# Squared tiles summed on VectorE, the first stage's products in column tiles, an earlier q copy, and head roots spread from rows

## The chip, the cores and the metric

The kernel runs on one core of one Trainium2 chip. The metric is the device time in microseconds (us) of one execution. Five engines have instruction streams of their own: PE (TensorE, matrix products), ACT (ScalarE), DVE (VectorE), POOL (GpSimd) and SP (SyncE, which here only issues transfers). They meet through semaphores: `then_inc` counts one up when an instruction is done, `wait_ge` holds an engine's stream until the count is reached.

## The reference

A sequence of 512 tokens of width 1024 goes through one large block and two smaller layers, all in float32:

```python
# block 1
mx = split(silu(c) @ w_ada + b_ada, 6); mc = the same of c_ctx
hx = modulate(rms_norm(x, g_pre_mix), mx[0], mx[1]);  hc = the same of ctx (256 tokens)
yx = concat(mlstm heads, silu(layer_norm(conv(ga * sigmoid(gb))))) @ w_out + b_out
x  = x + mx[2] * rms_norm(yx);  x = x + mx[5] * rms_norm(moe(modulate(rms_norm(x), mx[3], mx[4])))
# block 2, layers 0 (even) and 1 (odd)
for layer in range(2):
    x = x + mixer(rms_norm(x))            # rope attention, 8 pairs of heads; the odd one takes
                                          # rms_norm of each pair's output over 128 channels
    x = x + conv_ffn(rms_norm(x))         # (silu(gate) * val) @ w_down
return rms_norm(x, final_norm)
```

An `rms_norm` over the width needs, for each token, the sum of 1024 squares; the layer norm of the convolution needs a mean and a variance over 512 channels.

## The kernel before, in words

The program is a chain of stages with a barrier between them, and nothing of a stage's compute starts before the barrier; weights that `m.early` fetched are the exception. Activations lie turned: `m.x` is 8 tiles of 128 channels by 512 tokens, so a sum over channels is a matrix product with a constant matrix (`inv_d`, `inv_c`) that also spreads the result over all partitions. An ordinary weight product splits both sides in a high and a low part (`w_high`, `w_low`, `h_high`, `h_low`) and runs three passes of a faster format (`passes`); the sums of squares are plain float32 products, which the trace records as two matmuls each.

Five places matter here.

- `prologue` (lines 291 to 390). ACT squares the eight tiles of `x` and `ctx`; PE sums each pair as it comes (line 327). Then `product(n)`, four times, multiplies `silu_c` (two columns, for `c` and `c_ctx`) with a 2 MB quarter of `w_ada` that SP fetches (line 316), ACT copies the two rows out (line 363), `turn(n)` turns them into columns (line 340), and DVE adds the bias (line 381). Meanwhile DVE takes the reciprocal and scales `x` to `unit` tiles (line 376).
- `project_in` (lines 418 to 713). The last block of weight products is `rows("o")` in four chunks; after chunk 1 PE runs `mean` (line 518) and after chunk 2 `variance` (line 524), four float32 products each over the convolution's tiles `acc` and their centred squares `gb`.
- `Tail` (lines 2043 to 2083). Both `mix_out` (the output projection of an attention layer, eight columns `j` of 24 matmuls) and the second part of `conv_ffn` (eight columns of 30 matmuls) add their product to `m.x[:, j]` on DVE. `on_scalar` squares that tile, `on_tensor` adds the square into bank 6 or 7 two columns later, and `root` takes the square root at the stage's end. `split` says that the stage also prepares `hs.high` and `hs.low` for the next one.
- `mix_out` with `heads` (the odd layer). PE spreads the reciprocal roots `head_rstd` over the partitions (line 2186), DVE multiplies (`norm`, line 2152), ACT and DVE split, and only after all eight spreads does PE start the weight products (line 2198).
- `attention` (lines 2231 to 2605). Before the loop over eight pairs of heads the stage makes q, k and v of pair 0. All three projections write the same bank `BP`, so the projection of k waits until ACT has copied q out (`take(0, 0)`, line 2451, which signals `raw_done`). ACT has first to pass `act.wait_ge(w_in[1], 16)`, the arrival of the weights of the next pair, 1.5 MB that SP issues behind the 1 MB `amask`.

## Time and profile before

| | |
|---|---|
| median of 3 runs | 2568.27 us (2567.26 to 2576.4) |
| the profiled execution | 2567.37 us, of which the span from first to last instruction is 2565.6 us |
| busy in the span | PE 2357.6 us (92%), PE weight loads 1759.0 (69%), DVE 1535.2 (60%), ACT 1173.2 (46%), POOL 300.2 (12%) |
| mean granted TensorE clock | 0.955 of full speed (2.4 GHz; the lower level is 1.2 GHz) |

In the table of stretches each row gives the length, the busy time of each engine with its count of instructions, the granted clock, the busy share of the DMA engines and GB/s. A timeline row gives start, duration, engine, line, operation, output<-inputs, shapes and count; what stands in brackets is how long the engine had been idle before and who released it.

### The profile page before, as it was taken

How to read it: one execution, taken by the hardware profiler on the slowest of the kernel's cores; microseconds unless marked ns; L12 is line 12 of the kernel's file. 1: busy time of each engine (PE TensorE's matmuls, PEld its weight loads, DVE VectorE, ACT ScalarE, POOL GpSimd, SP SyncE). 2: the span in 40 equal slices, each digit the busy share in tenths (PEclk: the TensorE clock that was granted, in tenths of full speed). 3: DMA queues.
4: the chain of work that ended last, by engine and by line, in shares of the span. 5: the costliest groups of instructions: out<-in, count | busy, mean ns of one | idle time of the engine just before them, and what ended most of it. 6: DMA issues, size and time to landing. Idle time of an engine off the chain costs nothing. (4 is left out here: it accounts for less than half of the span.)

```text
span 2565.6 us, 30607 instructions
## 1 busy us (share of the span) xinstructions
PE 2357.6 (92%) x10686; PEld 1759.0 (69%) x10686; DVE 1535.2 (60%) x2414; ACT 1173.2 (46%) x1853; POOL 300.2 (12%) x223
## 2 busy tenths in 40 slices
PE   7998888899999999973899899999989979999997
PEld 2875664677677767752666578888767757888885
DVE  4974544777777777748455457637536544773663
ACT  4314442566666666644354434324334433442341
POOL 0000000121122112210343000000013410000000
PEclk9997899899999999996999899999999989999999
DMA  6203504799999999956421222222232101323221
GB/s 250 99 25 136 198 13 170 281 364 360 346 359 361 353 352 357 376 213 242 156 74 41 66 91 96 88 95 98 82 132 73 66 20 63 123 90 107 98 79 69
DMA packets 86753, 427.39 MB, mean 167 GB/s; under 512 B 19728, under 2 KB 19856, under 8 KB 51056
## 3 DMA queue, kind: packets, MB, share of 16 engines
q1 hardware_dynamic: 67344, 392.32, 41.9%
q0 software_dynamic: 19296, 33.60, 3.6%
q8 instruction: 66, 1.08, 0.2%
q14 instruction: 47, 0.39, 0.0%
HBM read 415.36 MB, written 38.80 MB: 177 GB/s over the span
## 5 line engine op out<-in xcount | busy, mean ns | idle before, releaser
L1796 DVE TENSOR_TENSOR w_gu_low<-raw,w_gu_high 128x1024 fp32r<-128x1024 f32 x264 | 322.6, 1223 | 121.9 <-ACT w_gu_high L1745 110.0
L1745 ACT ACTIVATE w_gu_high<-raw 128x1024 fp32r<-128x1024 f32 x264 | 279.8, 1060 | 108.7 <-PE banks L1701 107.8
L2718 PE MATMUL banks<-h_high,w_high 128*128 128x512 f32 x704 | 275.8, 392 | 6.8 <-DVE w_low L2818 6.8
L2718 PE MATMUL banks<-h_high,w_low 128*128 128x512 f32 x704 | 275.5, 391 | 0.0
L2718 PE MATMUL banks<-h_low,w_high 128*128 128x512 f32 x704 | 275.3, 391 | 0.0
L1713 PE MATMUL banks<-raw,act_t 128*128 128x512 f32 x528 | 237.6, 593 | 0.9 <-ACT act_t L1768 0.9
L1701 PE MATMUL banks<-w_gu_high,x_t_high 128*128 128x512 f32 x528 | 214.1, 406 | 2.0 <-DVE x_t_low L1803 2.0
L1701 PE MATMUL banks<-w_gu_high,x_t_low 128*128 128x512 f32 x528 | 208.0, 394 | 0.0
L1701 PE MATMUL banks<-w_gu_low,x_t_high 128*128 128x512 f32 x528 | 207.6, 393 | 0.0
L2745 ACT ACTIVATE w_high<-raw 128x2048 fp32r<-128x2048 f32 (+2 forms) x74 | 124.1, 1677 | 157.4 <-PE banks L2728 152.7
L2782 DVE TENSOR_TENSOR w_low<-raw,w_high 128x2048 fp32r<-128x2048 f32 (+2 forms) x74 | 148.3, 2004 | 59.6 <-ACT w_high L2745 59.5
L1713 PEld LDWEIGHTS banks<-raw,act_t 128*128 128x128 f32 x528 | 95.2, 190 | 95.8 <-issue 94.7
L2718 PEld LDWEIGHTS banks<-h_high,w_high 128*128 128x128 f32 x704 | 133.2, 189 | 36.1 <-issue 8.4
L2757 ACT ACTIVATE conv<-mix,vec 128x512 f32<-128x512 f32 x88 | 71.9, 817 | 183.2 <-DVE mix L2797 183.2
L2718 PEld LDWEIGHTS banks<-h_low,w_high 128*128 128x128 f32 x704 | 133.2, 189 | 27.7
L2718 PEld LDWEIGHTS banks<-h_high,w_low 128*128 128x128 f32 x704 | 133.0, 189 | 27.9
L1874 POOL DMA_INDIRECT x_rows<-h_rows,token_i x68 | 70.4, 1036 | 679.1 <-DVE token_i L1824 678.7
L2728 PE MATMUL banks<-hidden_high,w_high 128*128 128x512 f32 x352 | 141.7, 402 | 2.5 <-DVE w_low L2782 2.5
L2728 PE MATMUL banks<-hidden_high,w_low 128*128 128x512 f32 x352 | 137.2, 390 | 0.0
L2728 PE MATMUL banks<-hidden_low,w_high 128*128 128x512 f32 x352 | 137.0, 389 | 0.0
L1763 ACT ACTIVATE y_block<-banks 128x512 f32<-128x512 f32 x132 | 78.8, 597 | 86.4 <-PE banks L1713 85.7
L1701 PEld LDWEIGHTS banks<-w_gu_high,x_t_low 128*128 128x128 f32 x528 | 99.7, 189 | 22.7
(449 smaller groups left out, 4710.2 us busy)
## 6 DMA issues: line engine op xcount, KB each, us to landing
raw<-in_w_e SPq DMA_DIRECT2D x198, 1024.0 KB, 9.2
raw<-in_w_up SPq DMA_DIRECT2D x42, 1024.0 KB, 4.8
w_ada<-in_w_ada_later SPq DMA_DIRECT2D x16, 1024.0 KB, 5.3
expert_rows<-y_rows SPq DMA_DIRECT2D x16, 1024.0 KB, 11.4
raw<-in_w_down SPq DMA_DIRECT2D x16, 768.0 KB, 4.2
w_qkv<-in_w_even SPq DMA_DIRECT2D x7, 1536.0 KB, 6.5
w_qkv<-in_w_odd SPq DMA_DIRECT2D x7, 1536.0 KB, 6.5
raw<-in_w_down SPq DMA_DIRECT2D x16, 640.0 KB, 3.9
```

The lines of the kernel that those rows point to most:

```text
L1701: mm = pe.matmul(ps[:, BG, :], xp[:, k, :], wp[:, j, :], start=(k == 0 and i == 0), stop=(k == KT - 1 and i == 2))
L1713: mm = pe.matmul(ps[:, BY + n, :], at[:, k * P:(k + 1) * P], ex.chunk(GU + k, s)[:, half], start=(k == 0), stop=(k == 1))
L1745: act.activation(w_gu[c].high[:].rearrange("p j n -> p (j n)"), ex.chunk(c, s), ACT.Copy).then_inc(gu_high, 1)
L1763: act.activation(yb[s][:, n * 512:(n + 1) * 512], ps[:, BY + n, :], ACT.Copy).then_inc(y_out, 1)
L1796: dve.tensor_tensor(w_gu[c].low[:].rearrange("p j n -> p (j n)"), ex.chunk(c, s), w_gu[c].high[:].rearrange("p j n -> p (j n)").bitcast(F3 ...
L1874: pool.indirect_dma_start(xg[s][:], None, scratch["h_rows"], bass.IndirectOffsetOnAxis(ap=token_i[s][:, 0:1], axis=0), bounds_check=SEQ - ...
L2718: mm = pe.matmul(ps[:, 2 * s + c, :], wp[:, at:at + P], hp[:, k, :], start=(k == 0 and i == 0), stop=(k == KT - 1 and i == 2))
L2728: mm = pe.matmul(ps[:, 4 + s, :], wp[:, k * P:(k + 1) * P], hp[:, k, :], start=(k == 0 and i == 0), stop=(k == b - a - 1 and i == 2))
L2745: act.activation(w[s].high[:, 0:cols], raw[s][:, 0:cols], ACT.Copy).then_inc(high_done, 1)
L2757: act.activation(y[s][:, c, :], up[s][:, c, :], ACT.Identity, scale=tap(t, c, 2), bias=tap(t, c, 3)).then_inc(tap0, 1)
L2782: dve.tensor_tensor(w[s].low[:, 0:cols], raw[s][:, 0:cols], w[s].high[:, 0:cols].bitcast(F32), ALU.subtract).then_inc(low_done, 1)
```

## The change

Sums of squares: instead of one product for each squared tile, DVE adds the squared tiles and PE multiplies the total once. This is done in `prologue` (into `total`), in `mean` and `variance` of `project_in` (into `stat`), and in `Tail` (into `sq[0]`), so in both `mix_out` and both `conv_ffn` stages. The products of `prologue` are put in four column tiles of 32, one for each `k % 4`, and `turn` multiplies with the constant `quarters`, which also adds the four partial rows. In `attention` SP issues `weights(1)` ahead of `amask`, and ACT waits for it after the copy of q. In the odd `mix_out` the head roots are first transposed to eight rows, copied by ACT to `rows`, and each row is then spread by one product of 8 rows by 512 columns.

```diff
 # prologue
-                for k in range(KT):
-                    pe.wait_ge(sq_done, k + 1)
-                    for g, (t, n, sq) in enumerate(groups):
-                        mm = pe.matmul(ps[:, BS + g, 0:n], CONST.of(m.const, "inv_d"), sq[:, k, :], start=(k == 0), stop=(k == KT - 1))
+                pe.wait_ge(sq_added, KT - 1)
+                for g, (t, n, _) in enumerate(groups):
+                    mm = pe.matmul(ps[:, BS + g, 0:n], CONST.of(m.const, "inv_d"), total[:, t:t + n], start=True, stop=True)
...
-                        mm = pe.matmul(ps[0:2, BR + n, :], cs[:, k, :], w[n][:, k, :], start=(k == 0), stop=(k == KT - 1))
+                        at = 32 * (k % 4)
+                        mm = pe.matmul(ps[at:at + 32, BR + n, :], cs[:, k, :], w[n][:, k, :], start=(k < 4), stop=(k >= KT - 4))
...
-                        mm = pe.transpose(ps[:, BT, 2 * t:2 * t + 2], row[:, n, a * P:(a + 1) * P], CONST.of(m.const, "ident")[0:2, 0:2])
+                        mm = pe.matmul(ps[:, BT, 2 * t:2 * t + 2], row[:, n, a * P:(a + 1) * P], CONST.of(m.const, "quarters"), start=True, stop=True)
...
+                for k in range(1, KT):
+                    dve.wait_ge(sq_done, k + 1)
+                    if k >= 2:
+                        dve.wait_ge(sq_added, k - 1)
+                    for t, n, sq in groups:
+                        ins = dve.tensor_tensor(total[:, t:t + n], sq[:, 0, :] if k == 1 else total[:, t:t + n], sq[:, k, :], ALU.add)
+                    ins.then_inc(sq_added, 1)
 # project_in
-                    for c in range(4):
-                        mm = pe.matmul(ps[:, CB, :], CONST.of(m.const, "inv_c"), acc[:, c, :], start=(c == 0), stop=(c == 3))
-                    mm.then_inc(mean_done, 1)
+                    pe.matmul(ps[:, CB, :], CONST.of(m.const, "inv_c"), stat[:, 0, :], start=True, stop=True).then_inc(mean_done, 1)
...
                     if at == REST + 9:
+                        own(dve, dve.tensor_tensor(stat[:, 0, :], acc[:, 0, :], acc[:, 1, :], ALU.add))
+                        own(dve, dve.tensor_tensor(stat[:, 0, :], stat[:, 0, :], acc[:, 2, :], ALU.add))
                         low_w(19)
                 dve.wait_ge(dve_own, own.n)
-                dve.tensor_copy(m.scratch1[:, 0:1], acc[:, 0, 0:1]).then_inc(conv_made, 1)
+                dve.tensor_tensor(stat[:, 0, :], stat[:, 0, :], acc[:, 3, :], ALU.add).then_inc(conv_made, 1)
...
+                dve.wait_ge(conv_sq, 2)
+                own(dve, dve.tensor_tensor(stat[:, 1, :], gb[:, 0, :], gb[:, 1, :], ALU.add))
...
+                dve.tensor_tensor(stat[:, 1, :], stat[:, 1, :], gb[:, 3, :], ALU.add).then_inc(sq_summed, 1)
 # Tail
     def on_scalar(self, act, j):
         act.wait_ge(self.added, self.before + j + 1)
         if j >= 2:
-            act.wait_ge(self.summed, j - 1)
-        act.activation(self.sq[j % 2][:], self.x(j), ACT.Square).then_inc(self.sq_done, 1)
+            act.wait_ge(self.gathered, j - 1)
+        act.activation(self.sq[1 if j else 0][:], self.x(j), ACT.Square).then_inc(self.sq_done, 1)
...
+    def on_tensor(self, pe):
+        pe.wait_ge(self.gathered, KT - 1)
+        pe.matmul(self.m.ps[:, self.bank, :], CONST.of(self.m.const, "inv_d"), self.sq[0][:], start=True, stop=True).then_inc(self.summed, 1)
...
     def on_vector(self, dve, j):
+        if j >= 1:
+            dve.wait_ge(self.sq_done, j + 1)
+            if j >= 2:
+                dve.wait_ge(self.gathered, j - 1)
+            dve.tensor_tensor(self.sq[0][:], self.sq[0][:], self.sq[1][:], ALU.add).then_inc(self.gathered, 1)
 # mix_out, heads
+                    act.wait_ge(head_turned, 1)
+                    act.activation(rows[:].rearrange("h i t -> h (i t)"), ps[0:N_PAIR, 5, :], ACT.Copy).then_inc(rows_done, 1)
                     high(1)
...
+                    for i in range(TT):
+                        mm = pe.transpose(ps[0:N_PAIR, 5, i * P:(i + 1) * P], head_rstd[:, :, i], CONST.of(m.const, "ident"))
+                    mm.then_inc(head_turned, 1)
+                    pe.wait_ge(rows_done, 1)
...
-                        for i in range(TT):
-                            mm = pe.matmul(ps[:, 4 + 2 * (k % 2), i * P:(i + 1) * P], head_rstd[:, k, i:i + 1].broadcast_to([P, P]),
-                                           CONST.of(m.const, "ident"), start=True, stop=True)
-                        mm.then_inc(spread, 1)
+                        pe.matmul(ps[:, 4 + 2 * (k % 2), :], CONST.of(m.const, "ident")[0:N_PAIR, k:k + 1].broadcast_to([N_PAIR, P]),
+                                  rows[:].rearrange("h i t -> h (i t)"), start=True, stop=True).then_inc(spread, 1)
 # attention
+                sp.dma_start(weights(1), d[w_name][1]).then_inc(w_in[1], 16)
                 sp.dma_start(amask[:].rearrange("p a t -> p (a t)"), d["amask"]).then_inc(amask_in, 16)
-                sp.dma_start(weights(1), d[w_name][1]).then_inc(w_in[1], 16)
...
-                act.wait_ge(w_in[1], 16)
                 for part in range(3):
                     if part < 2:
                         take(0, part)
+                    if part == 0:
+                        act.wait_ge(w_in[1], 16)
                     high_part(1, 1, part)
```

On PE the first stage issued this before (the last pair of the sixteen sums, then products and turns; `k` is the tile that holds the context):

```order
L327 MATMUL banks<-mix,const 128x512
L327 MATMUL banks<-k,const 128x256
L333 MATMUL banks<-w_ada_5,silu_c 2x512 x16
L340 MATMUL banks<-const,v 128x2 x4
L333 MATMUL banks<-w_ada_5,silu_c 2x512 x8
```

and after the change this (`so` holds the total):

```order
L327 MATMUL banks<-so,const 128x512
L327 MATMUL banks<-so,const 128x256
L334 MATMUL banks<-w_ada_5,silu_c 32x512 x16
L341 MATMUL banks<-const,v 128x2 x4
L334 MATMUL banks<-w_ada_5,silu_c 32x512 x8
```

Two sums are left of sixteen, and the products write 32 partitions at a time.

On DVE the last columns of the even `mix_out` stood like this before:

```order
L2171 TENSOR_TENSOR x<-banks,x 128x512
L2148 TENSOR_TENSOR w_low<-w_out_15,w_high 128x1024
L2078 SCALAR_TENSOR_TENSOR h_low<-x,vec,h_high 128x512
L2171 TENSOR_TENSOR x<-banks,x 128x512
L2078 SCALAR_TENSOR_TENSOR h_low<-x,vec,h_high 128x512
L2171 TENSOR_TENSOR x<-banks,x 128x512
L2078 SCALAR_TENSOR_TENSOR h_low<-x,vec,h_high 128x512 x2
```

and now like this:

```order
L2192 TENSOR_TENSOR x<-banks,x 128x512
L2093 TENSOR_TENSOR tail_sq_15<-tail_sq_15 128x512
L2096 SCALAR_TENSOR_TENSOR h_low<-x,vec,h_high 128x512
L2192 TENSOR_TENSOR x<-banks,x 128x512
L2093 TENSOR_TENSOR tail_sq_15<-tail_sq_15 128x512
L2096 SCALAR_TENSOR_TENSOR h_low<-x,vec,h_high 128x512
L2093 TENSOR_TENSOR tail_sq_15<-tail_sq_15 128x512
L2096 SCALAR_TENSOR_TENSOR h_low<-x,vec,h_high 128x512
```

The addition of a square stands ahead of each `h_low`, and the last square's addition stands behind all the others.

On SP the start of the even attention stage was this:

```order
L2310 DMA rope<-in_rope 128x1024
L2307 DMA w_qkv_14<-in_w_even 128x1024
L2311 DMA amask<-in_amask 128x2048
L2312 DMA w_qkv_14<-in_w_even 128x3072
L257 DMA early<-in_w_eo 128x1024
```

and is now this:

```order
L2330 DMA rope<-in_rope 128x1024
L2327 DMA w_qkv_14<-in_w_even 128x1024
L2331 DMA w_qkv_14<-in_w_even 128x3072
L2332 DMA amask<-in_amask 128x2048
L257 DMA early<-in_w_eo 128x1024
```

Only the mask and the next pair's weights have changed places; the odd stage does the same. ACT's instructions stand in the same order as before and only its wait has moved.

## Rows read from the trace of the kernel before

**Rows 1.** Busy time by engine in two stretches, then TensorE clock, DMA share, GB/s.
```profile
1230.70:1236.00 5.30, 5.30 (x13) 4.14 (x14) 1.37 (x2) 0.75 (x1) 3.60 (x2) 0.50 0.21 50
...
2300.00:2566.00 266.00, 250.48 (x1087) 203.29 (x1085) 136.46 (x148) 81.22 (x84) 0.00 (x0) 0.98 0.26 88
```

**Rows 2.** Timeline of the first stage: start, duration, engine, line, operation.
```profile
14.48 0.40 ACT L356 ACTIVATE k<-x 128x256 f32<-128x256 f32 x1
...
20.01 13.89 PE L333 MATMUL banks<-w_ada,silu_c 128*2 128x512 f32 x32
...
26.19 0.69 DVE L376 TENSOR_TENSOR mix<-x,so 128x512 f32<-128x512 f32 x1
...
49.61 0.19 DVE L381 TENSOR_TENSOR mod<-banks,vec 128x32 f32<-128x32 f32 x1 [15.83 <-PE banks L340]
```

**Rows 3.** The transfers of `w_ada`, which line 316 issues.
```profile
L316 SPq DMA_DIRECT2D w_ada<-in_w_ada x4: 452/504/652, 5.8 to 7.6; - x4
DMA to landing us min/median/max: 13.0/19.4/25.9
```

**Rows 4.** Timeline of PE in the third stage.
```profile
224.33 1.94 PE L1043 MATMUL banks<-w_ada,silu_c 128*32 128x256 f32 x16 [4.24 <-DMA w_ada<-in_w_ada_later]
...
257.88 0.61 PE L1050 MATMUL banks<-const,mix 128*128 128x2 f32 x4
...
258.42 1.07 PE L1043 MATMUL banks<-w_ada,silu_c 128*32 128x256 f32 x16
```

**Rows 5.** Timeline at the convolution's mean and variance.
```profile
189.53 1.23 DVE L632 TENSOR_TENSOR w_low<-w_in,w_high 128x1024 fp32r<-128x1024 f32 x1 [6.89 <-ACT w_high L553]
...
192.24 0.15 DVE L705 COPY scratch<-mix 128x1 f32<-128x1 f32 x1
...
193.62 3.59 PE L518 MATMUL banks<-mix,const 128*128 128x512 f32 x8
...
197.25 2.48 DVE L708 TENSOR_TENSOR u<-mix,banks 128x512 f32<-128x512 f32 x4 [4.86 <-PE banks L518]
...
197.97 2.42 ACT L610 ACTIVATE mix<-u 128x512 f32<-128x512 f32 x4 [8.47 <-DVE u L708]
```

**Rows 6.** Timeline of the two output projections' columns and ends.
```profile
1462.17 0.69 DVE L2171 TENSOR_TENSOR x<-banks,x 128x512 f32<-128x512 f32 x1 [2.46 <-PE banks L2198]
...
1467.61 0.69 DVE L2171 TENSOR_TENSOR x<-banks,x 128x512 f32<-128x512 f32 x1 [3.06 <-PE banks L2198]
...
1498.41 0.69 DVE L2171 TENSOR_TENSOR x<-banks,x 128x512 f32<-128x512 f32 x1 [3.30 <-PE banks L2198]
...
1504.75 0.69 DVE L2171 TENSOR_TENSOR x<-banks,x 128x512 f32<-128x512 f32 x1 [4.99 <-PE banks L2198]
...
1505.67 0.63 ACT L2066 ACTIVATE tail_sq<-x 128x512 f32<-128x512 f32 x1 [5.09 <-PE banks L2072]
...
1508.22 0.69 ACT L2083 ACTIVATE rstd<-banks,const 128x512 f32<-128x512 f32 x1
...
2178.59 0.69 ACT L2083 ACTIVATE rstd<-banks,const 128x512 f32<-128x512 f32 x1 [0.60 <-PE banks L2072]
```

**Rows 7.** Timeline of PE at the start of both attention stages.
```profile
1230.65 0.77 PE L2338 MATMUL banks<-h_high,w_k_high 128*128 128x512 f32 x1 [4.49 <-ACT raw_q L2451]
...
1239.98 0.47 PE L2338 MATMUL banks<-h_high,w_v_high 128*128 128x512 f32 x1 [0.78 <-ACT raw_k L2451]
...
1899.47 0.76 PE L2338 MATMUL banks<-h_high,w_k_high 128*128 128x512 f32 x1 [4.41 <-ACT raw_q L2451]
...
1907.28 0.47 PE L2338 MATMUL banks<-h_high,w_v_high 128*128 128x512 f32 x1 [0.78 <-ACT raw_k L2451]
```

**Rows 8.** Timeline at the spreading of the head roots.
```profile
2116.91 10.82 PE L2186 MATMUL banks<-const,head_rstd 128*128 128x128 f32 x64 [3.03 <-DVE head_rstd L2158]
...
2119.02 0.75 DVE L2152 SCALAR_TENSOR_TENSOR mix<-mix,g,banks 128x512 f32<-128x512 f32 x1 [0.34 <-PE banks L2186]
```

**Rows 9.** Line 2498, one line of VectorE: duration in ns, least, median, most.
```profile
L2498 DVE TENSOR_TENSOR swapped_q<-swapped_q,rope x16: 677/1752/1782, 1234.6 to 2082.7; 128x512 f32<-128x512 f32 x16
```

More of the change, by code:

```diff
@@ L298, in prologue @@
         w = [sb(f"w_ada{n}", [P, KT, 512]) for n in range(N_FIRST)]
[L299 to L300 removed]
+        cs = sb("silu_c", [P, KT, 32])
+        row = m.v[:].rearrange("p i h n -> p (i h n)")[:, 0:N_FIRST * 512].rearrange("p (j n) -> p j n", j=N_FIRST)
         std = m.so[:].rearrange("p i n -> p (i n)")[:, 0:ALLT]
+        total = m.so[:].rearrange("p i n -> p (i n)")[:, ALLT:2 * ALLT]
         vec_in, const_in, rowv_in, w_in = sem("vec_in"), sem("const_in"), sem("rowv_in"), [sem(f"w_in{n}") for n in range(N_FIRST)]
         x_in = [sem(f"x_in{k}") for k in range(KT)]
[L304 to L305 removed]
+        silu_done, sq_done, ms_done, std_done, rstd_done, unit_done, parts_done, row_copied, product_done, mod_done, gain_done, cs_zero, sq_added = (
+            sem(s) for s in ("silu_done", "sq_done", "ms_done", "std_done", "rstd_done", "unit_done", "parts_done", "row_copied", "product_done", "mod_done", "gain_done", "silu_zero", "sq_added"))
         groups = [(0, SEQ, mix), (SEQ, CTX, m.hc)]
@@ L351, in _ @@
                 act.wait_ge(vec_in, 16)
-                act.activation(cs[:].rearrange("p k c -> p (k c)"), VEC.of(m.vec, "c"), ACT.Silu).then_inc(silu_done, 1)
+                act.wait_ge(cs_zero, 1)
+                act.activation(cs[:, :, 0:2], VEC.of(m.vec, "c").rearrange("p (k c) -> p k c", c=2), ACT.Silu).then_inc(silu_done, 1)
                 for k in range(KT):
@@ L362, in _ @@
                     act.wait_ge(product_done, n + 1)
-                    act.activation(row[:, n, :], ps[0:2, BR + n, :], ACT.Copy).then_inc(row_copied, 1)
+                    act.activation(row[:, n, :], ps[:, BR + n, :], ACT.Copy).then_inc(row_copied, 1)
                 act.wait_ge(gain_done, 1)
@@ L516, in mean @@
                     pe.wait_ge(conv_made, 1)
-                    for c in range(4):
-                        mm = pe.matmul(ps[:, CB, :], CONST.of(m.const, "inv_c"), acc[:, c, :], start=(c == 0), stop=(c == 3))
-                    mm.then_inc(mean_done, 1)
+                    pe.matmul(ps[:, CB, :], CONST.of(m.const, "inv_c"), stat[:, 0, :], start=True, stop=True).then_inc(mean_done, 1)
                 def variance():
-                    for c in range(4):
-                        pe.wait_ge(conv_sq, c + 1)
-                        mm = pe.matmul(ps[:, VB, :], CONST.of(m.const, "inv_c"), gb[:, c, :], start=(c == 0), stop=(c == 3))
-                    mm.then_inc(var_done, 1)
+                    pe.wait_ge(sq_summed, 1)
+                    pe.matmul(ps[:, VB, :], CONST.of(m.const, "inv_c"), stat[:, 1, :], start=True, stop=True).then_inc(var_done, 1)
                 for p, (name, j) in enumerate(PIECES[:V_AT]):
@@ L708, in _ @@
                     dve.tensor_tensor(centre[:, j, :], acc[:, j, :], ps[:, CB, :], ALU.subtract).then_inc(centred, 1)
+                dve.wait_ge(conv_sq, 2)
+                own(dve, dve.tensor_tensor(stat[:, 1, :], gb[:, 0, :], gb[:, 1, :], ALU.add))
+                dve.wait_ge(conv_sq, 3)
+                own(dve, dve.tensor_tensor(stat[:, 1, :], stat[:, 1, :], gb[:, 2, :], ALU.add))
+                dve.wait_ge(conv_sq, 4)
+                dve.tensor_tensor(stat[:, 1, :], stat[:, 1, :], gb[:, 3, :], ALU.add).then_inc(sq_summed, 1)
                 dve.wait_ge(std_done, 1)
@@ L2053, in __init__ @@
         self.added = sem("x_added") if added is None else added
-        self.sq_done, self.summed, self.high_done = (sem(n) for n in ("x_sq", "x_summed", "x_high"))
+        self.sq_done, self.gathered, self.summed, self.high_done = (sem(n) for n in ("x_sq", "sq_added", "x_summed", "x_high"))
     def gain(self, j):
@@ L2099, in mix_out @@
         tail = Tail(m, sb, sem, name, at, 7)
-        head_rstd, g = sb("head_rstd", [P, N_PAIR, TT]), sb("g", [P, 1])
-        head_root, head_ready, spread, normed = (sem(n) for n in ("head_root", "head_ready", "spread", "normed"))
+        head_rstd, g, rows = sb("head_rstd", [P, N_PAIR, TT]), sb("g", [P, 1]), sb("head_rows", [N_PAIR, TT, P])
+        head_root, head_ready, head_turned, rows_done, spread, normed = (
+            sem(n) for n in ("head_root", "head_ready", "head_turned", "rows_done", "spread", "normed"))
         NB = 4
@@ L2730, in job @@
                         mm.then_inc(used, 1)
-                        if part == 1 and j >= 2:
-                            tail.on_tensor(pe, j - 2)
                 pe.sem_inc(used, 1)
                 in_pairs(pe, job)
-                for j in range(KT - 2, KT):
-                    tail.on_tensor(pe, j)
+                tail.on_tensor(pe)
             @block.scalar
```

20 lines of the change are left out of this document (5 added, 15 removed).

## The prediction

> **What bounds the kernel now.** I looked first at the busy time by stretches [rows 1]: PE is busy for 250 of the last 266 us, and over the whole span for 92%. The chain that ended last is of no use here, for it follows only the last stage. So I went to the timelines of the five places that the change touches and asked each time what ended PE's idle time, since all stages stand behind one another with barriers between them: what a stage loses or gains goes into the span unless something else of the same stage ends late.
>
> In the first stage nothing but PE's products is on the path: 32 records take 13.89 us, 6.95 us a product, and DVE has been idle for 15.8 us when the last turned columns come at 49.61 [rows 2]. The transfers do not bound it: the last of the four is issued at 7.6 and lands at most 25.9 us later, at 33.5 [rows 3], while PE reaches its product only at 41.5. At the two normalisation sums of the convolution PE does 3.59 us of plain sums each time, between weight products that follow without a gap [rows 5]. In the output projections a column with a sum of squares behind it takes 1504.75 - 1498.41 = 6.34 us and one without 1467.61 - 1462.17 = 5.44 [rows 6]. At the start of the attention stages PE stands idle for 4.49 and 4.41 us ahead of the projection of k, until q is copied [rows 7].
>
> **The change part by part.**
>
> *First stage.* The sixteen sums become two. DVE must first add seven pairs; the last square is ready at 14.88, a 512 wide addition takes 0.69 [rows 2], a 256 wide one at most that. ACT's pairs come every 0.40 + 0.63 = 1.03 us [rows 2, 6], so the second is ready at 14.88 - 6 x 1.03 = 8.7 and the chain of seven ends by 8.7 + 7 x 1.4 = 18.5. With the two sums behind it (2.6 at twice the 0.86 per 512 columns below) the root comes by 21.5 at worst, 1.5 us later than the start of the products at 20.01 tells for now. The scaling of `x` ends at 49.61 - 15.83 = 33.78 and may be late by several us, as will be seen. So neither gain nor loss here. The products: the third stage has the same form at 256 columns, 16 records in 1.07 us at the full clock and 1.94 at the lower one [rows 4]. At 512 columns a product is then 2.1 or 3.9 us instead of 6.95, shorter than the spacing of the transfers (8 MB in about 20 us, 4.9 us each). The bound turns from PE to the fourth transfer. After 33.5 come one product (2.1 or 3.9), the turn of the third quarter beside ACT's copy of the fourth (0.7), and the last turn (0.61 [rows 4], or 1.1 at the lower clock): 37.0 or 39.6 for the addition that now starts at 49.61. A gain of 12.6 or 10.0; PE will have pauses of one or two us between its products, so I cannot say which level holds and take 11.0.
>
> By the Trainium skill (TensorE: Matmul & The Clock Gate, Part 3: Packing small matmuls, Measured speedup vs the span model), three column tiles of 32 at 512 columns gave 2.38 times the speed; the last product would then take 2.9 us and the gain would be 11.8 at the full clock. The rows of this kernel give 6.95 / 2.1 = 3.3 with four tiles, and the sum goes by them.
>
> *Mean and variance.* Eight records become two each time. Six of eight records go, three sums of a little under 0.9 us each, so 2.57 us, twice: 5.1. What may be late: the mean's total is two additions where DVE is idle for 6.89 us ahead of 189.53, and one of 0.69 in place of a copy at 192.24, done at 192.95, while PE comes at 193.62 [rows 5]. The variance's total: with the mean at 194.6 the four subtractions (2.48) end at 197.15 and ACT's squares (2.42, starting 0.72 behind) at 197.8; then come three additions, the first beside the last square, until about 199.4. PE's chunk of 24 matmuls (5.44 as in the columns above) runs from 194.5 to 199.9. It holds by half a microsecond; at worst 1 us is lost.
>
> *Tails.* Of eight sums per stage five lie between columns ahead of the end of the last one. They go: 5 x 0.90 = 4.5 in each of four stages (conv_ffn has the same sum behind columns of 30). What DVE has per column (0.69, 1.23 as in [rows 5], 0.69, 0.75 as in [rows 8], in all 3.35) fits in 5.44. At the end the chain gets longer. Now ACT squares the last tile 0.92 after the column's end (at 1504.75 as DVE sees it) and the root starts 3.5 after it in the even stage [rows 6], 2.8 in the odd one, where it waits for PE alone. After the change: addition of x 0.69, addition of the seventh square 0.69, square 0.63, addition 0.69, sum 1.0, with semaphores some 4.0. So 0.7 is given back in two stages and 1.2 in two, the first being those with a table load behind the square that covers part. Tails: 18.0 - 3.8 = 14.2.
>
> *Attention.* q is complete at 1230.65 - 4.49 = 1226.16; its copy may start there, and k's projection 0.78 later, which is the pause that PE has ahead of v's [rows 7]: 3.7 us earlier, in the odd stage 3.6. Next, the clock: after the long pause the granted clock is 0.50 up to 1236 [rows 1], and k's projection takes until 1239.98 - 0.78 = 1239.20, so 8.55 us, where v's, after the short pause, runs at full speed. In the odd stage k's takes 1906.50 - 1899.47 = 7.03. A projection at full speed is 5.7 (24 x 0.227 and the end). If the pause of 0.8 leaves the clock up, as it does ahead of v, 2.8 and 1.3 more are won. In sum 11.4, and 7.3 if the clock falls all the same. `weights(1)` arrives where it did less the mask, 1 MB or about 2.5 us, before ACT has to copy k. The mask is then last, 2.5 us later; DVE needs it ahead of the rotation of q, which has to be done only when k is. The projection of v follows k's and all of the loop follows it.
>
> *Head roots.* What is removed and added on PE is alike: 512 columns in plain float32 for each k. New on the path ahead of the first one are four transposes of 128 columns and ACT's copy of eight rows by 512. The first spread now takes from 2116.91 to 2119.02, 2.1 us for eight records [rows 8]; four transposes are bounded by half of that, the copy by the 0.69 of a root out of PSUM [rows 6], less the 0.34 for which alone DVE waits now. A loss of 0 to 2.5 us; I take 1.5, as the eight spreads then follow at DVE's pace as before.
>
> The sum: 11.0 + 5.1 + 14.2 + 11.4 - 1.5 = 40.2. The profiled execution took 2567.4 us (the span and 1.8 around it); this is 0.9 below the median. 2567.4 - 40.2 = 2527.2, as a median some 2527.5.
>
> **The rivals.**
>
> *The clock gives nothing back.* k's projection still starts low in both stages and the products of the first stage run at the lower level throughout: 4.1 + 1.0 less, 2532.5. For it speaks that every stage starts low [rows 1]; against it the short pause ahead of v.
>
> *Column tiles do not overlap here.* Then the first stage gives nothing, and 2538.5. The third stage's rows speak against it [rows 4], the same operation with the same constant.
>
> *The waits move.* The early q copy and the shorter tails meet another late party, say the swapped halves of q and k that DVE fetches through SP behind 3 MB of weights and mask. The two attention terms are then gone: 2539. Against it: the copy of q has a whole projection of k, over 5 us, for its way.
>
> *Slower.* DVE's operations on two tiles in SBUF can take 1.75 to 1.78 us where 0.68 is the least [rows 9]: a factor of 2.6. The new work of the tails is of that kind. DVE has 3.35 us of work in a column of 5.44, so it decides from a factor of 1.6 on; at 2.6 a column takes 8.7, and 28 columns of the four tails cost some 80 us, which makes 2609. What speaks against it: these long ones are beside POOL's own work, and POOL has no instruction in the tails of the last 266 us [rows 1], nor have the squares any in the others.
>
> **How the numbers follow.** The sum as it stands 0.62; no clock given back 0.20; tiles that do not overlap 0.05; waits that move 0.06; a still larger gain, with no loss at the head roots and the full clock in the first stage, below 2521, 0.04; slower 0.02; no change of more than 0.5%, by several terms failing at once, 0.01. A difference of 0.5% (12.8 us) is about what a measurement of this kernel can tell from no change. The unknown costs reach from 12.6 + 5.1 + 15 + 11.4 - 0 = 44.1 down to 10.0 + 4 + 12 + 7.3 - 2.5 = 30.8, so 2523 to 2537; with the first rival inside and the errors of several small terms the range is 2520 to 2537. Faster 0.95, same 0.03, slower 0.02.
>
> **What would show it.** In the profile of the changed kernel: the addition of the bias at 37 to 39.6 instead of 49.6, and PE waiting for a transfer of `w_ada` ahead of the last product; the convolution's root about 5.1 earlier in its stage, released by PE, and no PE idle time ahead of the variance; columns of `mix_out` at an even pitch of 5.44 and of `conv_ffn` at 6.8, with the root 4.0 to 4.2 after the last column; PE idle for about 0.8 ahead of k's projection, and that projection at 5.7; the first `norm` of the odd stage some 1.5 later after the barrier. The forecast is wrong by most if DVE's additions are longer than 0.7 or ACT's squares wait for them in every column, or if PE stands idle at the variance.

## The result, and the profile after

The changed kernel takes 2543.89 us (median of 4 runs, 2540.93 to 2546.25) against 2567.88 of the kernel before on the same chip (4 runs, 2567.26 to 2576.4): a ratio of 0.9898, 95% interval 0.9874 to 0.9923, 24 us or 1.0% faster. The prediction was 2527.5, with a range of 2520 to 2537: the direction was right, and the gain was three fifths of the forecast. The profiled execution of after took 2541.83 us, its span 2540.0, at a mean granted clock of 0.947 instead of 0.955.

The same ACT instructions stand in both traces. What they move by, from one mark to the next, tells where the time went; a small move of a stretch that no edit touches is called drift below:

| stretch (time of its end in the trace of before) | forecast | measured |
|---|---|---|
| first stage (49.6) | -11.0 | -10.6 |
| convolution and projections: mean and variance (212.2) | -5.1 | -5.1, beside -0.7 of drift |
| mixer, code unchanged (300.7) | 0 | **+8.3** |
| experts, up to the attention (1200) | 0 | -0.8 |
| attention, even and odd (1300; 1910) | -11.4 | -6.3 - 4.4 = -10.7 |
| output projection and convolution, even (1510; 1890) | -7.6 | -3.1 - 4.1 = -7.2 |
| start of the odd projection: head roots (2140) | +1.5 | **+7.1** |
| output projection and convolution, odd (2200; end) | -6.6 | -1.6 - 2.9 = -4.5 |
| rest | 0 | -1.4 |
| sum | -40.2 | -25.6 |

The sum is what the two profiled executions differ by. Two rows make most of the miss: the mixer and the head roots. Of the others the odd projection and convolution fall 2.1 short, and the rest are within 1.4. The first stage in the timeline of after (start, duration, engine, line, tile, shape, count, idle time before it and what ended it), which answers to [rows 2]:

```profile
16.94 2.90 PE L327 MATMUL banks<-so,const 128*128 128x512 f32 x4 [16.94 <-DVE so L379]
19.76 1.92 PE L334 MATMUL banks<-w_ada,silu_c 128*32 128x512 f32 x16
28.78 2.48 PE L334 MATMUL banks<-w_ada,silu_c 128*32 128x512 f32 x16 [1.99 <-DMA w_ada<-in_w_ada]
33.67 3.47 PE L334 MATMUL banks<-w_ada,silu_c 128*32 128x512 f32 x16 [0.61 <-DMA w_ada<-in_w_ada]
39.05 0.19 DVE L391 TENSOR_TENSOR mod<-banks,vec 128x32 f32<-128x32 f32 x1 [5.51 <-PE banks L341]
```

A product takes 1.92 us at the full clock and 3.47 where nearly all of it runs at the lower one; before it took 6.95 at the full clock, and PE waits for `w_ada`: the bound has turned to the transfers, and the addition of the bias stands at 39.05. Mean and variance are one product each, at 182.39 and 188.74, with no idle time of PE ahead of them. The attention's start answers to [rows 7]:

```profile
1218.34 0.47 PE L2358 MATMUL banks<-h_high,w_k_high 128*128 128x512 f32 x1 [0.78 <-ACT raw_q L2471]
...
1224.09 0.60 ACT L2471 ACTIVATE raw_k<-banks 128x512 f32<-128x512 f32 x1 [4.95 <-PE banks L2358]
```

PE pauses for 0.78 us instead of 4.49, and k's projection takes 5.75, at the full clock. In the tails the columns come every 5.44 us (1473.73, 1479.17) and in the even projection the root comes 4.85 after the last one (1484.61 to 1489.46); the forecast said 4.0 to 4.2. The head roots are another matter. The odd output projection in after, which answers to [rows 8]:

```profile
2088.73 1.02 PE L2204 MATMUL banks<-const,head_rstd 128*8 128x128 f32 x4 [3.04 <-DVE head_rstd L2179]
2089.78 0.59 ACT L2149 ACTIVATE head_rows<-banks 8x512 f32<-8x512 f32 x1 [0.61 <-PE banks L2204]
2090.42 14.02 PE L2210 MATMUL banks<-head_rows,const 8*128 8x512 f32 x16 [0.68 <-ACT head_rows L2149]
2095.94 0.75 DVE L2173 SCALAR_TENSOR_TENSOR mix<-mix,g,banks 128x512 f32<-128x512 f32 x1 [0.36 <-PE banks L2210]
2104.37 0.80 PE L2221 MATMUL banks<-h_high,w_high 128*128 128x512 f32 x1
2104.96 0.63 PE L2221 MATMUL banks<-h_low,w_high 128*128 128x512 f32 x1
```

Transposes and copy cost what was forecast, 1.7 us. But the eight spreads take 14.02 us instead of 10.82, DVE waits for each of them, and the first weight products take 0.63 instead of 0.39. The stretches of 4 us show why (length, busy time of PE, count, granted clock, share of the DMA engines, GB/s):

```profile
2092.00:2096.00 4.00, 4.00 (x6) 0.50 0.34 133
2096.00:2100.00 4.00, 4.00 (x6) 0.50 0.00 0
2100.00:2104.00 4.00, 4.00 (x6) 0.50 0.00 0
2104.00:2108.00 4.00, 4.00 (x10) 0.50 0.00 0
2108.00:2112.00 4.00, 4.00 (x18) 0.91 0.44 135
```

PE is busy all the time, and its granted clock stays at 0.50 (1.2 GHz) until the weight products have run for 4 us. In the trace of before the same stage, whose spreads come from 128 rows, is at 1.00 (2.4 GHz) from its second stretch on:

```profile
2117.00:2121.00 4.00, 4.00 (x20) 0.53 0.94 346
2121.00:2125.00 4.00, 3.80 (x31) 1.00 0.25 94
```

The mixer is a matter of the clock too. The stretch that holds its 640 products, in before and, below it, in after (length, busy time of PE, PEld, DVE, ACT and POOL, then clock and DMA):

```profile
212.00:309.35 97.35, 77.89 (x640) 53.82 (x640) 49.86 (x126) 41.23 (x122) 8.49 (x10) 0.81 0.50 185
```

```profile
195.70:301.00 105.30, 86.30 (x640) 59.59 (x640) 49.81 (x126) 40.75 (x122) 8.48 (x10) 0.75 0.46 171
```

The same instructions keep PE busy for 8.4 us more, DVE and ACT as long as before. In what follows "the mixer" is the time from ACT's table load ahead of it to the copy of the last of sixteen rows of the third stage: 212.20 to 300.66 in before, 88.46 us, and 195.90 to 292.70 in after, 96.80. The expectations give the longer stretch, 97.4 and 105.5; the differences agree within 0.3 us.

### The profile page after: what moved, and what is told of

Same layout as the page of the kernel before. It is cut to its first block and busy times, and to the rows that moved or that the text cites. A ratio compares the mean times of both kernels' runs of the same rounds, so it can differ in the third digit from the quotient of the medians.

```text
span 2540.0 us, 30442 instructions
## 1 busy us (share of the span) xinstructions
PE 2315.5 (91%) x10562; PEld 1740.4 (69%) x10562; DVE 1566.4 (62%) x2462; ACT 1175.5 (46%) x1854; POOL 299.0 (12%) x223
## 6 DMA issues: line engine op xcount, KB each, us to landing
raw<-in_w_e SPq DMA_DIRECT2D x198, 1024.0 KB, 10.8
```

## The experiments

Four questions: are the terms of the sum right one by one, what holds the clock down at the head roots, what lengthens the mixer, and does the answer give a better kernel.

**One part alone.** e3 is the kernel before with the first stage changed, e4 with mean and variance, e5 with the tails, e6 with the attention's start, e2 with the head roots; each takes its hunks of the diff as they stand.

> The kernel before with the change of the first stage alone (squares summed on VectorE, column tiles). The first stage ends 10.6 us earlier, as in the changed kernel: 2557. Theory A (the mixer's granted clock hangs on when it starts, or on what ran ahead of it): the mixer starts 10.6 us earlier with code that is unchanged, and its granted clock is that of the changed kernel or a third one, its length off by several us from 97.4. Rival B (the edit of the convolution's sums lengthens it, since PE is left with less to do at the end of the stage before): the mixer keeps its 97.4 us, and the gain is the whole 10.6. Rival C: chance between executions, any length, and a wide spread of the times.

> The kernel before with the sums of the convolution's mean and variance on VectorE alone. They come 5.1 us earlier: 2563. Theory A: the mixer starts 5.1 us earlier and has a length of its own, not necessarily longer. Rival B (this edit is what lengthens the mixer, by 8 us): 2571, slower than before, with the granted clock below 0.7 in the 20 us in which the state is copied and the first scores are made.

> The kernel before with the sums of squares of the four tails on VectorE alone. Each of the four stages was 1.6 to 3.7 us shorter in the changed kernel; alone they should give 3.8 + 3.8 + 3.3 + 3.3 = 14.2, or 12.9 if the even stages give 3.2 and 3.7 and the odd ones 3.1 and 2.9 as there: 2555. The mixer may take up to 8 us more or not, by the theory that its clock is chance; if such chance moves only the mixer, the four stages themselves give the same in every execution.

> The kernel before with the earlier copy of q and the moved load of the weights alone. By the wait that goes, 3.7 + 3.6, with the granted clock staying up in the projection of k (1.3 to 2.8 each): 11.4 to 12.3 us, 2556. Rival: the clock is not kept up and the gain is 7.3, 2560.

> The kernel before with the new spreading of the head roots alone. Theory A (few rows keep the clock at 0.50): 7 us slower than before, 2575; the granted clock is 0.50 from the transposes to 4 us or more after the first weight matmul. Rival B: the transposes and the copy alone, 1.5 to 2.5 us slower, 2570. The mixer of the third stage is at the same place as in the kernel before and keeps its length, 97.4 us from its first work to its last, if what lengthens it lies in the other parts; if it varies by chance, it may be some us longer here.

| | median (range, runs) | ratio, 95% | the part itself | mixer |
|---|---|---|---|---|
| e3 first stage | 2561.82 (2555.13 to 2567.39, 10) | 0.9969, 0.9955 to 0.9983 | -10.8 | +6.6 |
| e4 mean, variance | 2569.39 (2561.4 to 2573.42, 10) | 1.0, 0.9986 to 1.0014 | -5.1 | +8.6 |
| e5 tails | 2556.42 (2551.05 to 2560.23, 5) | 0.9937, 0.9917 to 0.9956 | -3.1 - 4.1 - 2.9 - 2.6 = -12.7 | 0.0 |
| e6 attention | 2554.58 (2553.01 to 2563.65, 5) | 0.9949, 0.9924 to 0.9974 | -6.6 - 4.9 = -11.5 | 0.0 |
| e2 head roots | 2580.94 (2575.17 to 2583.56, 6) | 1.0041, 1.0027 to 1.0056 | +7.6 | +8.1 |

Each part does in its own place about what it does in the changed kernel. Three of the five come within 0.2 us of their term, the tails give 1.5 less, and the head roots cost 6.1 more. In the last two columns the numbers come from one profiled execution each. The mixer is longer in three of the five, e2 among them, whose code is that of before up to the mixer and 1,800 us beyond, so a longer mixer needs none of the edits ahead of it.

**The head roots.** e1 is the changed kernel with the old spreads, four products of 128 columns from 128 rows for each head. e9 keeps the new ones and makes the tile that they read 128 rows high:

```diff
-        head_rstd, g, rows = sb("head_rstd", [P, N_PAIR, TT]), sb("g", [P, 1]), sb("head_rows", [N_PAIR, TT, P])
+        head_rstd, g, rows = sb("head_rstd", [P, N_PAIR, TT]), sb("g", [P, 1]), sb("head_rows", [P, TT, P])
...
+                    dve.memset(rows[:], 1.0).then_inc(rows_filled, 1)
...
-pe.matmul(ps[:, 4 + 2 * (k % 2), :], CONST.of(m.const, "ident")[0:N_PAIR, k:k + 1].broadcast_to([N_PAIR, P]),
+pe.matmul(ps[:, 4 + 2 * (k % 2), :], CONST.of(m.const, "ident")[:, k:k + 1].broadcast_to([P, P]),
```

> All of the change but the head roots: each of these is spread by four records of 128 columns from 128 rows, as before. Theory A (the few rows): products that use only 8 of TensorE's 128 rows leave the granted clock at 0.50, so that the spreads, and the first weight matmuls behind them, run at half speed; with 128 rows the clock is 1.00 within some 4 us of the stage's start, and the stage gives back the 7.1 us that the trace of the changed kernel shows: 2537 against 2543.9. Rival B (the pause): the clock falls at the barrier ahead of the stage and comes back a fixed time later whatever PE does; then only the transposes and ACT's copy are saved, 2.5 us, 2541.5. Rival C: the mixer's 8 us are chance, and the next execution has them back: then the mixer, in unchanged code, takes 8 us less here too, on top of either.

> The changed kernel with head_rows 128 rows high instead of 8: eight hold the turned roots, 120 hold ones that the zeros of the identity's columns take out again. The products are the same 512 columns each and the transposes and the copy stay; only the number of TensorE's rows in use differs, and a fill of 0.3 us on VectorE comes ahead. Theory A (few rows leave the granted clock low): the clock is 1.00 within some 4 us of the first product, the spreads take some 10.6 us instead of 14.0, the first weight matmuls 0.39 us each from the start, and the kernel is 5 us faster than the changed one, 2539. Rival B (the pause for ACT's copy or the transposes keep it low, or products of 512 columns in plain float32 do): 14 us again and 2544.

e1: 2533.92 us (2531.58 to 2536.46, 4 runs), ratio 0.9862 (0.9845 to 0.9878). Between the marks at 2116 and 2140 it loses nothing against before (-0.2), where after loses 7.1. Its mixer is 96.8 long again, which speaks against rival C. e9: 2538.67 us (2534.6 to 2539.93, 4 runs), ratio 0.9861 (0.9843 to 0.988) to its own runs of before. In its trace:

```profile
2090.82 1.02 PE L2206 MATMUL banks<-const,head_rstd 128*8 128x128 f32 x4 [3.53 <-DVE head_rstd L2181]
2092.52 10.78 PE L2212 MATMUL banks<-head_rows,const 128*128 128x512 f32 x16 [0.68 <-ACT head_rows L2150]
2103.37 0.40 PE L2223 MATMUL banks<-h_low,w_high 128*128 128x512 f32 x1
```

and in stretches of it:

```profile
2092.00:2096.00 4.00, 3.48 (x4) 0.50 0.77 288
2096.00:2100.00 4.00, 3.86 (x8) 0.88 0.00 0
2100.00:2104.00 4.00, 3.73 (x10) 1.00 0.00 0
```

Pause (0.5 us longer, by the filling of the tile), transposes, copy, columns and type are those of after; only 120 rows of ones, met by zeros, have been added, and the clock is up after 4 us. The start of the stage costs 2.2 us instead of 7.1. So the few rows held the clock down, and 5.0 of the 7.1 us are theirs; rival B is out.

By the Trainium skill (TensorE: Matmul & The Clock Gate, Part 1: The HAM clock gate, What's actually happening) the clock is released by how busy the engine has been. These rows show that busy in the profile's sense is not enough: 4.00 of 4.00 us at 0.50 with 8 rows in use, while with 128 rows it rose to 1.00 at 3.48 and 3.86 of 4.00.

**The mixer: chance, start or program.** r1 and r3 are the kernel before again, r2 and r4 the changed one; e7 and e8 were meant to move the mixer's start, by VectorE multiplications behind the convolution's root, two in e7 (on before) and four in e8 (on e1):

```diff
+for _ in range(2):
+    own(dve, dve.tensor_tensor(stat[:, 0, :], stat[:, 0, :], stat[:, 0, :], ALU.mult))
```

> The kernel before, unchanged, executed and profiled once more. If the mixer's 8 us are chance from one execution to the next (its start meets the changes of the granted clock at another instant), its length, 97.4 us in the first profile, may be another here, up to 106, and the execution longer by as much. If they come from the program (where its instructions and tiles lie), it is 97.4 again.

> The changed kernel, unchanged, executed and profiled once more. By chance the mixer takes anything from 97 to 106 us and the start of the heads keeps its loss of 7 us; by the program the mixer takes 105.5 again.

> The kernel before, unchanged, a third time. If the mixer's length is chance, it may be anything from 97 to 106 us here; three profiles of 97 would say that the kernel's own course brings it to the same place in nearly all executions.

> The changed kernel, unchanged, a third time. The mixer takes 105.5 us again if its start leads to it in nearly all executions, and another length if it is chance; the start of the heads is 7 us later than before in any case.

> The kernel before with two VectorE multiplications of 512 columns more behind the convolution's root, whose results nothing reads: the mixer starts some 1.3 us later, and nothing else differs. So far the mixer took 97.4 us in the four executions profiled in which it started within 0.3 us of the place in the first profile, and 104 to 106 in the six in which it started elsewhere, one of them only 1.2 us later. Theory A (the start decides): here too it takes some 8 us more, and the kernel 2577. Rival B (chance): it takes 97.4 or 105 whatever the start; rival C (the program's layout): 97.4, and 2569 for the kernel.

> The changed kernel with the old head roots, and four such multiplications (2.5 us) behind the convolution's root, so that the mixer starts 2.5 us later, 13.7 before the place of the first profile instead of 16.2. Theory A (the start decides, and the good places come again at some spacing): the mixer may fall back to 97.4 us; if so the kernel is 5.5 us faster than without the delay, 2528 against 2534, though it does more. Rival B (chance, or nothing but the start's being early): the delay costs its 2.5 us, 2536.5.

r1 2563.17 us, r3 2566.76, r2 2544.73, r4 2546.75, one run each. e7 2567.23 (2563.88 to 2571.71, 8 runs), ratio 0.9984 (0.9968 to 1.0001); e8 2535.63 (2531.72 to 2538.11, 5 runs), ratio 0.9847 (0.9831 to 0.9863). The delays failed as a tool: between the marks at 150 and 212 us e8 gains 6.63 us, exactly what e1 does, so the multiplications were hidden behind other engines; what start these two have comes from drift ahead. The starts (against before) and the mixer's length in all profiles whose mixer has the code of before:

| start moved by | mixer | kernels |
|---|---|---|
| -0.2 to +0.3 | 87.8 to 88.5 | before, r1, r3, e5, e6 |
| +0.4 | 91.7 | e7 |
| +1.2 | 96.6 | e2 |
| -5.7, -11.5 | 97.1, 95.1 | e4, e3 |
| -13.7 to -17.9 | 96.8 to 97.0 | after, r2, r4, e1, e8, e9 |

Three profiles each of before and after give each its own length every time, within 0.7 us, so the difference between the two is not chance from one execution to the next. The length goes with the place at which the stage starts only roughly. Between before and e2 1.2 us go with a mixer 8.1 us longer, but r4 starts 1.4 us later than after, and e8 2.6 us later, with the same length. That it is the place at all, and not where the program's instructions lie, is argued and not shown, since the delays did not move the start.

Nor does the instant at which the clock first falls in the stage order the lengths by itself. By the granted clock in the traces it is 2.7 to 4.0 us behind the stage's start in the five profiles of 88 us, 4.2 in e7, 4.4 in e2 and 1.4 to 1.6 in the six of the last row, but 3.2 in e3, whose mixer takes 95.1. What sets the long mixers apart is a later fall. In the five of 88 us the clock is at 1.00 from 33 to 35 us behind the start until the work ends; in e7 it falls again at 38.3, in e4 at 39.6, in e2 at 38.6 and 55.6, in after at 38.9 and 56.0. Within an execution the loss is these falls of the clock. In after, in stretches of 2 us:

```profile
247.00:249.00 2.00, 2.00 (x19) 1.00 0.57 98
249.00:251.00 2.00, 2.00 (x22) 1.00 1.00 426
251.00:253.00 2.00, 1.41 (x14) 0.72 0.26 82
253.00:255.00 2.00, 2.00 (x18) 0.50 0.96 369
```

and some of what PE did there, in rows ahead of the fall at 251.9 and behind it:

```profile
247.71 1.98 PE L1089 MATMUL banks<-g_rows,sel 36*128 36x512 f32 x4
249.62 0.61 PE L1064 MATMUL banks<-const,mix 128*128 128x2 f32 x4
250.16 1.07 PE L1057 MATMUL banks<-w_ada,silu_c 128*32 128x256 f32 x16
251.82 0.94 PE L1064 MATMUL banks<-const,mix 128*128 128x2 f32 x4 [0.59 <-ACT mix L831]
256.38 3.00 PE L1107 MATMUL banks<-state,entering_q 64*128 64x129 f32 x13
```

Ahead of the fall stand spreads from 36 rows, products of 2 columns and column tiles. In before the same series runs through at 1.00 from 259 to 267, and its row takes 1.61 instead of 3.00:

```profile
267.07 1.61 PE L1093 MATMUL banks<-state,entering_q 64*128 64x129 f32 x13
```

So the same series can run through or let the clock fall. If it is the rows that make the difference, it is the head roots' cause once more.

**More rows, more work.** e10 puts products of 128 rows into PE's idle time, e11 makes the tiles behind the twelve spreads 96 rows high, e12 does both; all three on top of e1. e13 and e14 are e11's edit alone on the changed kernel and on the kernel before.

```diff
 # the lines that matter; each pair of lines stands in a place of its own
 # e10: behind the transposes of the keys fill(2), behind the first part of the third stage fill(1)
+pe.matmul(ps[:, B_A, :], CONST.of(m.const, "ident"), m.k[:, 0, 0:SEQ], start=True, stop=True)
 # e11: g_rows and running_most are sb(..., [SUMS, SEQ]) and filled, g and most their first 36 rows
-pe.matmul(ps[:, 3 + n % 2, :], SELS.of(sel, "pair", n * P, P)[0:ROWS_N], e_rows[:], start=True, stop=True)
+pe.matmul(ps[:, 3 + n % 2, :], SELS.of(sel, "pair", n * P, P), most_wide[:], start=True, stop=True)
-pe.matmul(ps[:, B_G[r], :], SELS.of(sel, "unit", (r * H_M + h) * P, P)[0:ROWS_N], g[:], start=True, stop=True)
+pe.matmul(ps[:, B_G[r], :], SELS.of(sel, "unit", (r * H_M + h) * P, P), g_wide[:], start=True, stop=True)
```

> The changed kernel with the old head roots, and three products of 128 rows by 512 columns put into PE's idle time at the start of the mixer (two behind the transposes of the keys, where PE waits 4.2 us for the weights, one behind the first part of the third stage, where it waits 2.4): their results are overwritten. Theory A (the granted clock follows how much of TensorE is in use, and the mixer's loss is nothing but the clock): it rises some 10 to 20 us earlier in the mixer, which takes 97 us or less instead of 105, and the kernel takes 2526 or less against 2534. Rival B (the fillers only delay what follows): 2 to 3 us slower, 2537.

> The changed kernel with the old head roots, and the twelve spreads of the mixer (running_most and g_rows, 36 rows high, by selectors) made 96 rows high: the further rows of the tiles hold ones or zeros, those of the selectors are zero, so the results are the same and the products have the same 512 columns. Theory A (few rows in use let the granted clock fall while PE is busy, as at the heads): the falls at 20 to 60 us of the mixer, which now come at or behind such spreads, are fewer, and the mixer takes 97 to 99 us instead of 105: 2527 against 2534. Rival B (the clock falls by the instant at which the stage meets it, whatever the spreads' rows): 105 still, and 2534, or 2535 with the longer fill of the tiles.

> Both the 96 rows of the mixer's spreads and the three fillers in PE's idle time. With the fillers alone the clock was 1.00 from 7 to 24 us of the mixer, fell in the 3 us in which PE has little to do, came back and fell once more right behind four spreads of 36 rows; the mixer took 102.6. Theory A: the fall behind the spreads goes, the mixer takes 95 to 98 us and the kernel 2526 or less. Rival B: nothing over the fillers alone, 2531 to 2534.

> The changed kernel, heads and all, with the mixer's twelve spreads 96 rows high. Theory A (the 36 rows let the granted clock fall while PE is busy): the mixer takes some 98 us instead of 105.5, the heads keep their loss, and the kernel takes 2536 against 2544. Rival B: what the edit brought together with the old head roots had to do with these, or with where the stage began, and 2544 stays.

> The kernel before with the mixer's spreads 96 rows high. Theory A: its mixer keeps 97 to 98 us in every execution, where until now some had a longer one: the upper end of its times, 2572 to 2577, is seen less, the fastest stay at 2563 to 2566, and the median falls by 0 to 4 us. Rival B: no change, 2568 and the same spread.

| | median (range, runs) | ratio, 95% | start | mixer |
|---|---|---|---|---|
| e10 e1 and fillers | 2533.86 (2528.48 to 2542.67, 5) | 0.9847, 0.9822 to 0.9871 | -18.0 | 93.6 |
| e11 e1 and 96 rows | 2527.1 (2524.54 to 2531.57, 5) | 0.9834, 0.9815 to 0.9852 | -14.4 | 89.8 |
| e12 e1 and both | 2523.86 (2519.54 to 2529.15, 5) | 0.982, 0.98 to 0.984 | -14.3 | 86.9 |
| e13 after and 96 rows | 2535.04 (2531.71 to 2537.32, 4) | 0.986, 0.9834 to 0.9886 | -17.0 | 89.8 |
| e14 before and 96 rows | 2567.04 (2563.71 to 2569.24, 10) | 0.9984, 0.9971 to 0.9997 | +1.2 | 89.7 |

Two pairs settle that most of the loss hangs on the 36 rows. e2 and e14 start the mixer at the same place, 1.2 us late, and the clock first falls 4.4 and 4.3 us behind the start: 96.6 us with 36 rows and 89.7 with 96. e13 and after differ by that edit alone: 89.8 and 96.8, and the kernel 2535 instead of 2544. In e11, e13 and e14 the clock is back 35 us behind the mixer's start, as in after and e2, and then stays up until PE runs out of work at the mixer's end. e2, in stretches of 8 us from 32 us behind the start of the mixer on:

```profile
245.20:253.20 8.00, 8.00 (x52) 0.71 0.39 131
253.20:261.20 8.00, 8.00 (x48) 0.65 0.38 132
261.20:269.20 8.00, 7.40 (x80) 0.99 0.40 132
269.20:277.20 8.00, 8.00 (x46) 0.50 0.76 265
277.20:285.20 8.00, 7.40 (x60) 0.87 0.33 117
```

and e14 in the same ones:

```profile
245.20:253.20 8.00, 8.00 (x55) 0.80 0.37 131
253.20:261.20 8.00, 8.00 (x85) 1.00 0.36 133
261.20:269.20 8.00, 7.41 (x78) 1.00 0.67 241
269.20:277.20 8.00, 7.40 (x69) 1.00 0.70 267
```

The runs of e14 all lie below 2569.3, while 7 of the 13 of before beside them lie between 2571.8 and 2576.2: it may be that in the kernel before, too, the upper half of the times is such falls. That is not shown, since none of the three profiles of before is of an execution above 2568 us.

The fillers alone are inconclusive in the median. In the trace they do what was expected up to 220 us: the clock is up early. It then falls a first time where PE has little to do (busy for 1.43 of the 2 us ahead of 220), is back at 226.6, and falls again under the 36 rows while PE never pauses. e10, in stretches of 1 and 2 us, with the products that lie there:

```profile
228.00:229.00 1.00, 1.00 (x7) 1.00 0.00 0
229.00:230.00 1.00, 1.00 (x3) 0.98 0.00 0
230.00:232.00 2.00, 2.00 (x5) 0.50 0.00 0
```

```profile
226.80 1.98 PE L1073 MATMUL banks<-running_most,sel 36*128 36x512 f32 x4
228.83 2.65 PE L1073 MATMUL banks<-running_most,sel 36*128 36x512 f32 x4
```

In e12 the clock comes back at 230.5, again right ahead of these eight products. From 96 rows they take 1.98 and 1.98, and the clock stays up:

```profile
230.60 1.98 PE L1077 MATMUL banks<-running_most,sel 96*128 96x512 f32 x4
232.88 1.98 PE L1077 MATMUL banks<-running_most,sel 96*128 96x512 f32 x4
```

```profile
232.00:234.00 2.00, 2.00 (x9) 1.00 0.00 0
234.00:240.00 6.00, 6.00 (x51) 1.00 0.43 149
```

e12 is the fastest kernel of the study: 1.8% below before, and 0.8% below the changed kernel by their ratios (0.982 to 0.9898).

## Why the prediction was wrong, step by step

- *First stage, 11.0:* the mechanism was right, and 10.6 came of it. The bound turned to the fourth transfer (forecast at 33.5, seen at 33.67). Four column tiles overlap by 3.6 (6.95 / 1.92, both at the full clock), so that the rival in which they do not overlap is out. Only the last product counts, and it ran at the lower clock. The terms for that case add up to 39.2 (33.5 + 3.9 + 0.7 + 1.1) and not to the 39.6 that the prediction has, and the measured time is 39.05. So the case was the lower bound, and the middle value came near it by some luck.
- *Mean and variance, 5.1:* right, 5.1 in after and in e4. PE never waited, so the half microsecond of room was enough.
- *Tails, 14.2:* the mechanism was right, the size 2.5 too large: 12.7 in e5, 11.7 in after. The pitch was 5.44 as said; the term that was off is the end of the chain. It was forecast at 4.0 to 4.2 and took 4.85 us from the last column to the root in the even stage, and in the odd one 4.9 in after, where the last sum met a lower clock, and 4.1 in e1. The odd stage of after falls another 0.8 short of e1's. That lies behind the root, at the start of the next stage: between 3 and 7 us behind the first weight product the clock is at 0.71 in after (2161 to 2165) and at 0.92 in e1 (2156 to 2160).
- *Attention, 11.4:* near enough, 10.7 in after and 11.5 in e6; the clock stayed up behind the short pause, so that the rival in which the clock gives nothing back is out for this term, and of the waits that move nothing is seen. The argument for the former, that every stage starts low, does not hold of the first stage: there the clock is at 1.00 from 11 to 49.6 us in the trace of before.
- *Head roots, 1.5, bounded by 0 and 2.5:* **this step failed.** The steps that were priced, transposes and copy, took 1.7 us, and 2.2 in e9 with the filling of its tile. What failed was "the eight spreads then follow at DVE's pace as before", which rested on "what is removed and added on PE is alike: 512 columns in plain float32 for each k". The columns are alike, the rows are 8 instead of 128, and with 8 the granted clock stayed at 0.50: 7.1 us at the start of the stage in after, 7.6 in e2, 2.2 in e9. Of the 7.1, 1.7 are transposes and copy and 3.2 the longer spreads (14.02 instead of 10.82); the weight products behind them, at the lower clock for 4 us, make up the rest.
- *The sum:* **this step failed too.** It let a stage's gain go into the span unless something else in the same stage ended late. It had no term for stages whose code is unchanged but whose clock runs another course. The mixer took 8.3 us more in after; with 96 rows in its spreads it took 1.2 to 1.4 more than in before (part of which is the filling of the tiles), at the three starts that were seen.
- *The rival "slower":* additions of 2.6 times their length were not seen (0.68 and 0.69 in the tails of after). Its 80 us also do not follow from its figures: 14 columns at 8.7 instead of 5.44 and 14 at 8.7 instead of 6.8 make 72.

Both failed steps together are 5.6 + 8.3 = 13.9 us of the 14.6 between the sum and the trace. The tails' 2.5, the attention's 0.7 and the first stage's 0.4 are about made up by 2.9 of drift elsewhere. Taking both losses away gives 2527.1 (e11), the number forecast. That it agrees so well is partly luck: e11 has the old head roots and so pays none of the 1.5 that the forecast has for the new ones, which about makes up for its longer mixer. None of the rivals had either loss in it. One of them asked about the clock, but only at the attention's start and in the first stage, and not at the heads or in stages whose code stays.

What stays open: by what rule rows, columns and time make the clock fall, why the change brings the mixer to falls that it did not meet before, and why a kernel comes to the same ones each time that it was profiled. No run here varies the columns alone.

## What to carry to other kernels

Where a product is put in place of another, compare the rows that it keeps in use and not only its columns: if it stands in a stretch without full products, at a stage's start above all, filling it up with rows that meet zeros can keep the clock. It cost PE nothing here (four records of 512 columns take 1.98 us from 36 rows and from 96, both at the full clock), and filling the tiles cost other engines 0.5 us at the heads and at most 1.4 in the mixer. A part's gain can be taken back in a stage that it doesn't touch, so compare unchanged stages too, and look at the granted clock of a stretch before looking for a wait. Here a PE that was busy for longer, with the same instructions and as fully as before, had lost clock and not gained work.

## What the runs showed of the hardware

- Products from 8 rows kept PE busy for 14 us without a pause, at a granted clock of 0.50 throughout; the same from 128 rows reached 1.00 after some 4 us and took 10.8 (e9).
- The clock fell from 1.00 to 0.50 in the middle of a fully busy stretch, under products from 36 rows (e10 at 230 us), and did not under the same products from 96 (e12 at 230 to 240 us).
- The longest length of one unchanged stage was 1.11 times its shortest (97.1 in e4, 87.8 in r1), with a start 5.6 us earlier.
- Rows that meet zeros in the other operand still count for the clock: in e9 ones in 120 of 128 rows, with zeros as their weights, brought it from 0.50 to 1.00.
